# Latent attention in pairs of steps: rotary score products of both steps together, and part of the output projection between the last two turnings

## The reference

```
def mla_mixer(h, k, v, w_q_a, q_a_norm, w_q_b, q_norm, w_out, cos, sin):
    q = (rms_norm(h @ w_q_a, q_a_norm) @ w_q_b).reshape(B, T, MLA_HEADS, QK_NOPE + QK_ROPE)
    q = rms_norm(q, q_norm)
    q = jnp.concatenate([q[..., :QK_NOPE], apply_rope(q[..., QK_NOPE:], cos, sin)], axis=-1)
    scale = (QK_NOPE + QK_ROPE) ** -0.5
    ...
        s = jnp.einsum('bqhd,bkhd->bhqk', qb, k).astype(jnp.float32) * scale
        p = masked_softmax(s, kpos[None, :] <= t[:, None])
        o = jnp.einsum('bhqk,bkhd->bqhd', p.astype(v.dtype), v)
    ...
    return o @ w_out
```

## Time and profile before

| | |
|---|---|
| time, median of 3 runs | 2112.38 us (2111.87 to 2113.69) |
| the profiled execution's own time | 2109.97 us |
| its span, first to last instruction | 2108.2 us |
| PE busy | 2053.9 us (97%) |
| DVE busy | 1447.2 us (69%) |
| ACT busy | 967.5 us (46%) |
| granted TensorE clock, mean | 0.994 |
| latent attention, first score matmul to output projection | 802.56 to 862.72 us |

### The profile page before, as it was taken

The page is one execution under the profiler, slowest core; times in us unless marked ns, Lnnn a source line. Parts: engine busy times, 40 slices in busy tenths (PEclk is TensorE's granted clock), DMA queues, the critical chain, the costliest instruction groups (busy, mean ns, idle before and its releaser), DMA issues. The chain is left out here.

```text
span 2108.2 us, 37701 instructions
## 1 busy us (share of the span) xinstructions
PE 2053.9 (97%) x15185; PEld 1765.7 (84%) x15185; DVE 1447.2 (69%) x2825; ACT 967.5 (46%) x1869; POOL 129.6 (6%) x121
## 2 busy tenths in 40 slices
PE   8999999999999999999999999999999999899997
PEld 8997777899988977889998877878887788688886
DVE  5247865988864687589887457666666666685566
ACT  5337972555400367445551015534443444466554
POOL 1113320000000300000000002000000000020000
PEclk9999999999999999999999999999999999999998
DMA  5230001332332321122323221211111111112211
GB/s 184 81 140 21 2 2 61 106 104 101 107 125 75 108 71 41 41 90 86 116 101 114 96 89 55 80 69 60 60 60 60 60 60 54 44 60 81 81 41 41
DMA packets 30667, 159.37 MB, mean 76 GB/s; under 512 B 3393, under 2 KB 3905, under 8 KB 17857
## 3 DMA queue, kind: packets, MB, share of 16 engines
q1 hardware_dynamic: 30240, 157.24, 21.3%
q10 hardware_dynamic: 288, 0.20, 0.0%
HBM read 155.33 MB, written 2.10 MB: 75 GB/s over the span
## 5 line engine op out<-in xcount | busy, mean ns | idle before, releaser
L224 PE MATMUL ps<-late_parts,panel_upper 128*128 128x256 f32 (+1 forms) x1376 | 459.6, 334 | 0.0
L223 PE MATMUL ps<-late_parts,panel_upper 128*128 128x256 f32 (+1 forms) x1260 | 432.6, 343 | 2.5 <-issue 1.8
L225 PE MATMUL ps<-late_parts,panel_parts 128*128 128x256 f32 (+1 forms) x1260 | 425.1, 337 | 0.0
L219 DVE TENSOR_TENSOR panel_parts<-panel_sb,panel_upper 128x512 fp32r<-128x512 f32 (+1 forms) x334 | 328.1, 1010 | 14.0 <-ACT panel_upper L731 8.4
L223 PE MATMUL ps<-panel_upper,hT_parts 128*128 128x256 f32 (+2 forms) x964 | 296.0, 307 | 7.7 <-DVE h_lower L926 7.7
L225 PE MATMUL ps<-panel_upper,h_lower 128*128 128x256 f32 (+2 forms) x964 | 283.9, 295 | 0.0
L224 PE MATMUL ps<-panel_parts,hT_parts 128*128 128x256 f32 (+2 forms) x964 | 282.7, 293 | 0.0
L224 PEld LDWEIGHTS ps<-late_parts,panel_upper 128*128 128x128 f32 x1376 | 259.4, 189 | 25.9 <-issue 0.2
L223 PEld LDWEIGHTS ps<-late_parts,panel_upper 128*128 128x128 f32 x1260 | 237.5, 188 | 32.5 <-issue 2.4
L225 PEld LDWEIGHTS ps<-late_parts,panel_parts 128*128 128x128 f32 x1260 | 238.7, 189 | 28.8
L223 PE MATMUL ps<-hT_parts,panel_upper 128*128 128x512 f32 (+1 forms) x508 | 202.1, 398 | 4.2 <-DVE h_lower L3439 2.5
(11 more groups left out here) (541 smaller groups left out, 3705.9 us busy)
## 6 DMA issues: line engine op xcount, KB each, us to landing
panel_sb<-ffn_gate_up_w SPq DMA_DIRECT2D x76, 512.0 KB, 4.5
panel_sb<-gdn_w SPq DMA_DIRECT2D x24, 1024.0 KB, 4.8
panel_sb<-ffn_down_w SPq DMA_DIRECT2D x22, 1024.0 KB, 4.8
panel_sb<-nsa_w SPq DMA_DIRECT2D x13, 1024.0 KB, 6.1
panel_sb<-gla_w SPq DMA_DIRECT2D x12, 1024.0 KB, 4.9
panel_sb<-gdn_out_w SPq DMA_DIRECT2D x8, 1024.0 KB, 4.8
panel_sb<-ffn_gate_up_w SPq DMA_DIRECT2D x6, 1024.0 KB, 4.9
panel_sb<-nsa_out_w SPq DMA_DIRECT2D x4, 1024.0 KB, 5.0
```

The source lines that it names most:

```text
L219: return engine.tensor_tensor(out, src, hi.bitcast(F32), ALU.subtract)
L223: mm(out, w_hi, x_hi, start=start, stop=False, skip_group_check=skip_group_check)
L224: mm(out, w_hi, x_lo, start=False, stop=False, skip_group_check=skip_group_check)
L225: return mm(out, w_lo, x_hi, start=False, stop=stop, skip_group_check=skip_group_check)
```

## The change

All three queues take the steps two at a time. PE computes the plain scores of steps v and v+1, then the rotary products of both; then turn, values, turn, values. DVE does both weightings, then up to two lower_o, a lower_out, both biased, a lower_out. ACT is reordered to match. Buffers become four. In the tail, heads 0 to 5 of out(0) stand between turn(14) with values(13) and turn(15), and those of out(1) between values(14) and values(15).

```diff
--- before.py
+++ after.py
@@ -1842,11 +1842,11 @@
     k_ss, k_inv, k_mul, kr_mul = [take(TT, MH) for _ in range(4)]
     q_ss, q_ssr, q_inv, q_ninv = [take(TT, MH) for _ in range(4)]
     qn_gain = take(1)
-    mmin, mbias, msum = [[take(2) for _ in range(3)] for _ in range(3)]
+    mmin, mbias, msum = [[take(2) for _ in range(4)] for _ in range(3)]
     zst = qTn[:, :, :].rearrange("p h t -> p (h t)")[:, 0:TT * 704].rearrange("p (t n) -> p t n", t=TT)
     staging = [hT[:, 5, :], hT[:, 6, :], hT[:, 7, :], h_raw[:, 5, :]]
     rope_b = h_raw[:, 6, :]
-    mprob = [hT[:, 2 * b:2 * b + 2, :] for b in range(3)]
+    mprob = [hT[:, 2 * b:2 * b + 2, :] for b in range(4)]
     mpT = [h_raw[:, 2 * b:2 * b + 2, :] for b in range(2)]
     QK = NOPE + ROPE
     LQ, LKV = Q_LORA, KV_LORA + ROPE
@@ -2028,25 +2028,25 @@
         turn_heads(6 * TT - 3)
 
         def scores(v):
-            pair, t, n = m_step(v)
             if v == 0:
-                pe.wait_ge(S("m_dve_saved"), TT + 1)
-                pe.wait_ge(S("m_q_out"), TT + 1)
-            elif v == 1:
                 pe.wait_ge(S("m_dve_saved"), TT + 2)
                 pe.wait_ge(S("m_q_out"), TT + 2)
             else:
-                pe.wait_ge(S("m_biased"), v - 1)
+                pe.wait_ge(S("m_biased"), v)
             if v == 2 * TT:
                 pe.wait_ge(S("m_dve_saved"), 2 * TT)
-            for ab in range(2):
-                mm(ps[:, 2 * (v % 2) + ab, 0:n], qTn[:, 2 * pair + ab, tokens(t)], kTn[:, 2 * pair + ab, 0:n], start=True, stop=False, skip_group_check=True)
-            for c in range(0, n, SPAN):
-                keys = slice(c, min(c + SPAN, n))
+            for u in (v, v + 1):
+                pair, t, n = m_step(u)
                 for ab in range(2):
-                    r = slice(ab * ROPE, (ab + 1) * ROPE)
-                    last = mm(ps[:, 2 * (v % 2) + ab, keys], qTr[r, pair, tokens(t)], kTr[r, pair, keys], start=False, stop=True, skip_group_check=True)
-            last.then_inc(S("m_scores"), 1)
+                    mm(ps[:, 2 * (u % 2) + ab, 0:n], qTn[:, 2 * pair + ab, tokens(t)], kTn[:, 2 * pair + ab, 0:n], start=True, stop=False, skip_group_check=True)
+            for u in (v, v + 1):
+                pair, t, n = m_step(u)
+                for c in range(0, n, SPAN):
+                    keys = slice(c, min(c + SPAN, n))
+                    for ab in range(2):
+                        r = slice(ab * ROPE, (ab + 1) * ROPE)
+                        last = mm(ps[:, 2 * (u % 2) + ab, keys], qTr[r, pair, tokens(t)], kTr[r, pair, keys], start=False, stop=True, skip_group_check=True)
+                last.then_inc(S("m_scores"), 1)
 
         def turn(v):
             pair, t, n = m_step(v)
@@ -2058,7 +2058,7 @@
                 pe.wait_ge(S("m_pT"), v)
             for ab in range(2):
                 for kt in range(t + 1):
-                    last = nc.tensor.transpose(ps[:, 4 + ab, tokens(kt)], mprob[v % 3][:, ab, tokens(kt)], ident[:])
+                    last = nc.tensor.transpose(ps[:, 4 + ab, tokens(kt)], mprob[v % 4][:, ab, tokens(kt)], ident[:])
             last.then_inc(S("m_prob_turned"), 1)
 
         def values(v):
@@ -2078,15 +2078,14 @@
         pe.wait_ge(S("m_act_saved"), 4 * TT)
         turn_heads(6 * TT - 2)
         scores(0)
-        scores(1)
         turn_heads(6 * TT - 1)
-        for v in range(M_STEPS):
-            if v + 2 < M_STEPS:
-                scores(v + 2)
+        for v in range(0, M_STEPS - 2, 2):
+            scores(v + 2)
             turn(v)
-            if v >= 1:
+            if v:
                 values(v - 1)
-        values(M_STEPS - 1)
+            turn(v + 1)
+            values(v)
 
         def out(n, heads):
             slot, i = mla_slot(P_OUT + n // 2)
@@ -2101,9 +2100,15 @@
             slot, i = mla_slot(P_OUT + q)
             split_ready(pe, slot, i)
             if q == 0:
+                turn(M_STEPS - 2)
+                values(M_STEPS - 3)
                 pe.wait_ge(S("m_o_split"), M_STEPS - TT)
-                for n in range(2):
-                    out(n, range(0, MH - 2))
+                pe.wait_ge(S("m_biased"), M_STEPS)
+                out(0, range(0, MH - 2))
+                turn(M_STEPS - 1)
+                values(M_STEPS - 2)
+                out(1, range(0, MH - 2))
+                values(M_STEPS - 1)
                 pe.wait_ge(S("m_o_split"), M_STEPS)
                 for n in range(2):
                     out_done(out(n, range(MH - 2, MH)), n)
@@ -2220,8 +2225,8 @@
             act.wait_ge(S("m_biased"), v + 1)
             for ab in range(2):
                 h = 2 * pair + ab
-                last = nc.scalar.activation(mprob[v % 3][:, ab, 0:n], mprob[v % 3][:, ab, 0:n], ACT.Exp, bias=mbias[v % 3][:, ab:ab + 1],
-                                            scale=q_ninv[:, t, h:h + 1], accum_out=msum[v % 3][:, ab:ab + 1])
+                last = nc.scalar.activation(mprob[v % 4][:, ab, 0:n], mprob[v % 4][:, ab, 0:n], ACT.Exp, bias=mbias[v % 4][:, ab:ab + 1],
+                                            scale=q_ninv[:, t, h:h + 1], accum_out=msum[v % 4][:, ab:ab + 1])
             last.then_inc(S("m_exp"), 1)
 
         def turned(v):
@@ -2244,14 +2249,22 @@
             nc.scalar.copy(hi_ring[slot][:, rows, :], ring[slot][:, rows, :]).then_inc(S("m_out_upper"), 1)
 
         exps(0)
-        for v in range(M_STEPS):
-            if v + 1 < M_STEPS:
-                exps(v + 1)
+        exps(1)
+        for v in range(0, M_STEPS, 2):
+            if v:
+                if v > 2:
+                    upper_o(v - 3)
+                upper_o(v - 2)
+            upper_out(v)
             turned(v)
-            if v >= 1:
-                upper_o(v - 1)
-            upper_out(v)
-        upper_o(M_STEPS - 1)
+            if v + 2 < M_STEPS:
+                exps(v + 2)
+            turned(v + 1)
+            if v + 2 < M_STEPS:
+                exps(v + 3)
+            upper_out(v + 1)
+        for v in range(M_STEPS - 3, M_STEPS):
+            upper_o(v)
         mla_passed(act_panels)
 
     def query_std(act, b):
@@ -2423,20 +2436,20 @@
         def biased(v):
             pair, t, n = m_step(v)
             wait_apart(dve, "m_scores", v + 1)
-            if v >= 3:
-                wait_apart(dve, "m_prob_turned", v - 2)
+            if v >= 4:
+                wait_apart(dve, "m_prob_turned", v - 3)
             for ab in range(2):
-                last = nc.vector.tensor_tensor_reduce(out=mprob[v % 3][:, ab, 0:n], in0=ps[:, 2 * (v % 2) + ab, 0:n], in1=causal[:, T - n:T], scale=1.0, scalar=3e38,
-                                                      op0=ALU.add, op1=ALU.min, accum_out=mmin[v % 3][:, ab:ab + 1])
+                last = nc.vector.tensor_tensor_reduce(out=mprob[v % 4][:, ab, 0:n], in0=ps[:, 2 * (v % 2) + ab, 0:n], in1=causal[:, T - n:T], scale=1.0, scalar=3e38,
+                                                      op0=ALU.add, op1=ALU.min, accum_out=mmin[v % 4][:, ab:ab + 1])
             link(last)
-            nc.vector.tensor_tensor(mbias[v % 3], mmin[v % 3], q_inv[:, t, 2 * pair:2 * pair + 2], ALU.mult).then_inc(S("m_biased"), 1)
+            nc.vector.tensor_tensor(mbias[v % 4], mmin[v % 4], q_inv[:, t, 2 * pair:2 * pair + 2], ALU.mult).then_inc(S("m_biased"), 1)
 
         def weighted(v):
             pair, t, n = m_step(v)
             dve.wait_ge(S("m_exp"), v + 1)
-            link(nc.vector.reciprocal(msum[v % 3], msum[v % 3]))
+            link(nc.vector.reciprocal(msum[v % 4], msum[v % 4]))
             for ab in range(2):
-                last = nc.vector.tensor_scalar(mprob[v % 3][:, ab, 0:n], mprob[v % 3][:, ab, 0:n], msum[v % 3][:, ab:ab + 1], None, ALU.mult)
+                last = nc.vector.tensor_scalar(mprob[v % 4][:, ab, 0:n], mprob[v % 4][:, ab, 0:n], msum[v % 4][:, ab:ab + 1], None, ALU.mult)
             last.then_inc(S("m_weighted"), 1)
 
         def lower_o(v):
@@ -2459,17 +2472,21 @@
         biased(1)
         query_scale(1)
         save(5 * TT + 3)
-        for v in range(M_STEPS):
+        for v in range(0, M_STEPS, 2):
             weighted(v)
+            weighted(v + 1)
+            if v:
+                if v > 2:
+                    lower_o(v - 3)
+                lower_o(v - 2)
+                lower_out(v - 1)
             if v + 2 < M_STEPS:
                 biased(v + 2)
-            if v >= 2:
-                lower_o(v - 2)
-            if v:
-                lower_out(v - 1)
+                biased(v + 3)
+            lower_out(v)
         lower_out(M_STEPS - 1)
-        lower_o(M_STEPS - 2)
-        lower_o(M_STEPS - 1)
+        for v in range(M_STEPS - 3, M_STEPS):
+            lower_o(v)
 
         def out_ready(n):
             if n % 2:
```

## The result

The changed kernel takes 2114.95 us (median of 15 runs, 2112.04 to 2119.93) where the kernel before takes 2112.38 (15 runs, 2109.72 to 2114.73). The ratio is 1.0017, with a 95% interval of 1.0009 to 1.0024: slower by 2.6 us on the medians, more than the interval leaves to chance, and inside the 0.2% that I had called no change. The forecast was 2115.5. The two profiled executions, both at a mean granted clock of 0.994, took 2109.97 and 2113.02: 3.05 us apart. Most of the scatter goes with that mean clock: the changed kernel's executions at 0.994 took 2112.0 to 2113.0, the four at 0.989 took 2119.6 to 2119.9.

What follows compares the result with a forecast made beforehand. PE was taken to set the pace, busy 59.3 of the attention's 60.2 us. Terms -2.25 + 0.66 + 1.8 + 1.9 - 0.3 + 1.25 gave +3.1 us, 2115.5 on the 2112.38 median; range 2110.8 to 2118.

Steps and rivals of the forecast that it cites:

- later first scores: Start of the attention: scores(0) now waits for the second late save instead of the first, +0.66 us.
- wait at scores(2): Start: scores(2) now waits for biased(1), not only biased(0), so PE waits 1.8 us.
- waits for the copy (steps 1, 3, 9, 11): Inside pairs: turn(v+1) waits for ACT's copy of turn(v); +0.62 at the first pair, +0.15 twice, +0.17 at v = 8.
- waits before scores(4), scores(12): Two later pairs: plain scores wait for biased of the pair's second step, +0.4 us twice.
- old waits gone (first turning, tail): Old PE waits vanish: 0.3 us at the first turning, 1.0 together at turn(14) and turn(15).
- wait at values(13): Tail: values(13) waits for the bank lower_o(11) frees, now later in the DVE and ACT queues, +1.15 us.
- wait ahead of heads 6 and 7: Tail: final heads' matmuls stand right behind values(15), so splitting its output is uncovered, +1.1 us.
- changes of mode, with turns behind values: All pairs: fewer full/half-height changes save 2.55 us, turns right behind values add 0.3; together -2.25 us.
- Turns behind values: turn(v+1) right behind values(v-1), six times before the tail, at +0.05 us each, 0.3 in all.
- Rival 1: Whole attention: new waits overlap or hide, savings stay; -3.9 us, 2108.5; decided at scores(2); 12%.
- Rival 2: DVE and ACT become the bound, each of 7 rounds about 0.3 us later; +5 us, 2117.5; 21%.
- Rival 3: New waits of 1.8 and 1.1 us drop the clock to 1.2 GHz; +3.1 + 10 us, 2125; 4%.

Runs made afterwards that it cites:

- e2: The changed kernel with each plain product waiting only for its own banks (step v for biased(v-2), v+1 for biased(v-1)); ratio to the kernel before 1.0003.
- e9: e6 with upper_o of output 13 ahead of the copy of turn(15), and turn(v) between plain and rotary products; ratio to the kernel before 0.9980.
- e5: The kernel before with only the tail of the change; ratio to the kernel before 0.9998.
- e10: The kernel before with out(0, heads 0 to 5) between values(13) and turn(15), and out(1) left behind values(15); ratio to the kernel before 0.9998.
- e3: The changed kernel with the output of odd steps split one round earlier on ACT and DVE; ratio to the kernel before 1.0017.
- e7: e6 with the rotary products of each step right behind its own plain scores; ratio to the kernel before 1.0013.
- e4: The changed kernel with out(1, heads 0 to 5) behind values(15) instead of ahead of it; ratio to the kernel before 1.0014.
- e6: The changed kernel with the edits of e2, e3 and e4 together, and scores(0) and scores(1) singly as before; ratio to the kernel before 1.0000.

## Why the prediction was right

The sum was +3.1 us and D grew by 2.97; the mechanism was shown part by part. That the total is nearer than its parts is in part luck: errors of 0.3 to 0.7 us in the smaller terms cancel. Each term, forecast and measured:

| term | forecast | measured | shown by |
|---|---|---|---|
| later first scores | +0.66 | +0.66 | start rows |
| wait at scores(2) | +1.8 | +1.7 | start rows, e2 |
| waits for the copy (steps 1, 3, 9, 11) | +1.1 | +1.5 | distances in the timeline, most of it by e9 |
| waits before scores(4), scores(12) | +0.8 | +0.8 | e2 |
| old waits gone (first turning, tail) | -1.3 | -1.3 | tail rows, e5, e10 |
| wait at values(13) | +1.15 | +1.1 | e3 |
| wait ahead of heads 6 and 7 | +1.1 | +1.08 | tail rows, e5 |
| changes of mode, with turns behind values | -2.25 | -2.5 | the rest of the sum |

- *The copy.* I took 0.06 for every handover. From VectorE to PE it is mostly that (807.45 to 807.51); from the end of the copy on ScalarE to turn(1) it is 0.14 (813.28 to 813.42). Four waits came out 0.1 larger each for it.
- *Turns behind values.* I gave them +0.05 each, between 0 and 0.1. They cost up to 0.07 less than behind rotary products (0.65 against 0.71 for six transposes), near 0.4 us less in all where I had 0.3 more.
- *Starting again after a wait.* I counted a wait as its idle time alone. The plain scores of 7 units take 3.20 us where they follow a wait (807.51 to 810.71; the same at 814.64 and 843.53) and 3.10 where they don't:

```profile
836.28 3.17 PE L2041 MATMUL ps<-late_sb 128*128 128x384 f32 x8
839.38 1.79 PE L2048 MATMUL ps<-arena_sb 64*128 64x256 f32 x16
```

That is 0.10 more for each of the three waits for biased. With the 0.4 too little for the copy, it cancels the error of the turns.
- *Rival 1* (the waits hide) fell at scores(2), as it said it would: they start 1.9 us late. Its other half is true of a better order: e9 has the savings without the bill. *Rival 2* (side engines) did not come: of the value waits of steps 3, 5 and 11, where it was to be decided, PE has none. *Rival 3* (the clock): 1.00 throughout the attention, with waits up to 1.7 us. Elsewhere the clock does fall: in the trace of the kernel before, TensorE ran 32 matmuls of one column from 1834.27 and stood idle from 1838.0 to 1839.71; in that idle time the granted clock fell from 1.00 to 0.50, the level of 1.2 GHz, and stayed there to 1849. Matmuls of 512 columns start 0.43 us apart in that stretch and 0.23 behind it. So the rival's price, 10 us at half the clock, does occur in this kernel, and the prediction's "no fall at a wait of this length" is true of the earlier trace rows and not of the whole trace. (The Trainium skill, "TensorE: Matmul & The Clock Gate", Part 1, has an idle engine fall to 1.2 GHz; the trace agrees at 1839 us, and no wait of the attention shows it.)
- That a change of tiling mode drains TensorE (the Trainium skill, "TensorEngine Tiling (Array Packing)", Key Properties) agrees with e7: 0.40 us for one change each way more. By itself it would have forecast a gain, and the change is slower.
- *What I missed on the way* is in e4: I had followed the semaphores of the changed order and not asked which bank out(1) had been covering once it moved.

What stays open: the last row of the table is what remains of the sum. Read from the rows it is -0.40 for the first pair, seven times -0.30, near -0.4 for the turns, +0.3 for the starts after waits and +0.15 in the tail (the first matmuls of values(13) and of out(1)), -2.45 together; 0.1 is left. And the +0.66 of the start was not undone alone, only together with the single first steps in e6.

## What to carry to other kernels

Grouping steps to save changes of mode also groups their waits: give each half of a group its own wait for its own banks, or the group starts when the later of them is ready. When work that covered a latency is moved, list every buffer whose release it covered, and the queue places ahead of each release on the other engines; two of the waits of over 1 us here (values(13) in the change, values(15) in e4 and e6) were only such places. A cover for a copy can be had for little from independent matmuls of the same array mode: the turning between plain and rotary products won 1.14 us here.

## What the runs showed of the hardware

- Going from full-height to half-height matmuls costs 0.12 us and back 0.20 ahead of transposes, 0.30 ahead of plain matmuls (e7); it is the same for 128 and for 512 columns. In e9, where transposes and no change of mode follow the plain scores of 7 units, 0.05 is left over instead of 0.14 (806.13 to 809.14 is 3.01, 836.28 to 839.38 in the change 3.10).
- A group of plain matmuls that starts after a wait for a semaphore takes 0.10 us more than one that starts without (3.20 and 3.10 for 7 units at 1.00 clock).
- A handover to PE takes 0.06 us from VectorE (807.45 to 807.51, 873.90 to 873.96), once 0.15 (861.37 to 861.52), and 0.14 from ScalarE's copy.
